# Block-diagonal gate products of a recurrent mixer: two products a tile instead of three, and an earlier place in TensorE's queue

## What is computed

```python
def rglru_mixer(x, w_in, conv_w, conv_b, w_a, b_a, w_x, b_x, a_param, w_out):
    z = x @ w_in
    gate_branch, xb = z[..., :D_RNN], z[..., D_RNN:]
    xp = jnp.pad(xb, ((0, 0), (CONV_WIDTH - 1, 0), (0, 0)))
    xc = conv_b + conv_w[0] * xp[:, 0:S]
    for k in range(1, CONV_WIDTH):
        xc = xc + conv_w[k] * xp[:, k:k + S]
    xh = xc.reshape(B, S, LRU_HEADS, LRU_HEAD_DIM)
    r = jax.nn.sigmoid(jnp.einsum('bshi,hij->bshj', xh, w_a).reshape(B, S, D_RNN) + b_a)
    ig = jax.nn.sigmoid(jnp.einsum('bshi,hij->bshj', xh, w_x).reshape(B, S, D_RNN) + b_x)
    log_a = -LRU_C * r * jax.nn.softplus(-a_param)
    a = jnp.exp(log_a)
    mult = jnp.sqrt(-jnp.expm1(2.0 * log_a))
    bterm = mult * (ig * xc)
    _, h = lax.associative_scan(_lin_combine, (a, bterm), axis=1)
    y = h * jax.nn.gelu(gate_branch)
    return y @ w_out
```

## Time and profile before

| | |
|---|---|
| median of three executions | 1741.39 us |
| the profiled execution, its own time | 1741.45 us |
| its span, first to last instruction | 1739.6 us |
| mean granted TensorE clock | 0.999 |
| PE busy | 1728.8 us (99%), 9535 matmul instructions |
| PE weight load busy | 1500.2 us (86%) |
| DVE busy | 1262.9 us (73%) |
| ACT busy | 1003.7 us (58%) |
| POOL busy | 58.9 us (3%) |
| moved by DMA | 311.65 MB, mean 179 GB/s |

### The profile page before, as it was taken

One profiled execution on the slowest core, in us unless ns is written; L12 is line 12 of the kernel. 1 busy time (PEld: TensorE's weight loads), 2 busy tenths in 40 slices (PEclk: granted clock), 3 DMA queues, 4 the chain that ended last, 5 costly groups with the idle time before them and its releaser, 6 DMA issues.

```text
span 1739.6 us, 24239 instructions
## 1 busy us (share of the span) xinstructions
PE 1728.8 (99%) x9535; PEld 1500.2 (86%) x9535; DVE 1262.9 (73%) x1602; ACT 1003.7 (58%) x1247; POOL 58.9 (3%) x95
## 2 busy tenths in 40 slices
PE   9999999999999999999999999999999999999998
PEld 8888998888888888888889888888888988888887
DVE  6766777766677666876667898867666898876665
ACT  7544566654467444754457866464446966565444
POOL 7200000000000000000001000000000000000000
PEclk9999999999999999999999999999999999999999
DMA  7755435665545655465545544356555554446552
GB/s 244 255 189 188 162 122 170 217 222 189 191 169 181 212 187 176 144 208 185 189 145 194 184 165 145 122 186 220 190 192 170 163 176 134 138 165 215 188 186 88
DMA packets 211564, 311.65 MB, mean 179 GB/s; under 512 B 6434, under 2 KB 166112, under 8 KB 211360
## 3 DMA queue, kind: packets, MB, share of 16 engines
q1 hardware_dynamic: 207472, 303.84, 53.4%
q0 software_dynamic: 3712, 6.44, 1.2%
q10 hardware_dynamic: 304, 0.33, 0.1%
HBM read 309.54 MB, written 1.05 MB: 179 GB/s over the span
## 4 chain that ended last, share of the span: by engine, by line
PE 91%; ACT 4%; DVE 3%; issue 1%; DMA 0%; SPq 0%; DVEq 0%; ACTq 0%
PE psD L1945 28%; PE psA L1834 27%; PE psA L1839 14%; PE psA L1912 3%; PE psA L1927 3%; PE psA L1778 3%; PE psA L1945 2%; PE psD L2231 2%; PE psA L1931 1%; PE psA L1916 1%; PE psA L1783 1%; PE psA L2015 1%; ACT hi L455 1%; PE psD L2168 1%; PE psD L2015 1%
## 5 line engine op out<-in xcount | busy, mean ns | idle before, releaser
L927 DVE TENSOR_TENSOR lo<-raw,hi 128x2048 fp32r<-128x2048 f32 x285 | 650.5, 2290 | 171.9 <-ACT hi L455 171.2
L455 ACT ACTIVATE hi<-raw 128x2048 fp32r<-128x2048 f32 x285 | 542.4, 1909 | 77.2 <-PE psD L1945 33.5
L1834 PE MATMUL psA<-xT,hi 128*128 128x512 f32 x2094 | 501.1, 390 | 0.1
L1834 PEld LDWEIGHTS psA<-xT,hi 128*128 128x128 f32 x2094 | 387.2, 188 | 77.0 <-DVE xT L960 0.3
L1839 PEld LDWEIGHTS psA<-xT,lo 128*128 128x128 f32 x2112 | 271.9, 191 | 11.8 <-issue 0.5
L1839 PE MATMUL psA<-xT,lo 128*128 128x256 f32 x2112 | 276.8, 283 | 0.1
L1945 PE MATMUL psD<-hi,prod_hi 128*128 128x512 f32 x544 | 213.4, 392 | 0.0
L1945 PE MATMUL psD<-hi,prod_lo 128*128 128x512 f32 x544 | 212.6, 391 | 0.0
L1945 PE MATMUL psD<-lo,prod_hi 128*128 128x512 f32 x544 | 143.6, 389 | 0.0
L593 ACT ACTIVATE scr<-psA 128x512 f32<-128x512 f32 x66 | 39.3, 595 | 163.3 <-PE psA L1839 163.3
L608 ACT ACTIVATE prod_hi<-scr 128x512 fp32r<-128x512 f32 x66 | 41.7, 632 | 157.8 <-DVE scr L1309 157.8
(11 more groups left out here) (308 smaller groups left out, 1926.2 us busy)
## 6 DMA issues: line engine op xcount, KB each, us to landing
raw<-in_w_in SPq DMA_DIRECT2D x48, 1024.0 KB, 5.2
raw<-in_ffn_w_up SPq DMA_DIRECT2D x43, 1024.0 KB, 5.4
raw<-in_ffn_w_gate SPq DMA_DIRECT2D x43, 1024.0 KB, 5.4
raw<-in_ffn_w_down SPq DMA_DIRECT2D x43, 1024.0 KB, 5.0
raw<-in_w_gate SPq DMA_DIRECT2D x22, 1024.0 KB, 5.3
raw<-in_w_up SPq DMA_DIRECT2D x22, 1024.0 KB, 5.3
raw<-in_w_down SPq DMA_DIRECT2D x22, 1024.0 KB, 4.9
raw<-in_lru_w_in SPq DMA_DIRECT2D x10, 1024.0 KB, 5.3
```

The source lines that it names most:

```text
L455: act.activation(hi[:, n % RING, :], raw_of(n), ACT.Copy).then_inc(hi_ready, 1)
L927: dve.tensor_tensor(lo[:, n % RING, :], raw_of(n), hi[:, n % RING, :].bitcast(F32), ALU.subtract).then_inc(lo_ready, 1)
L1834: pe.matmul(psA[:, bank + f, :], w_hi[:, k, f * P:(f + 1) * P], xT[:, k].rearrange("p e s -> p (e s)"), start=(k == 0), stop=False)
```

## The change

The band now holds, for each output tile, two sets of rows instead of three. The product of the tile with itself stands in one set (parity m % 2), and in the other set lie the blocks of both neighbours, in one 128-row weight: a head's block keeps the rows at which its input features lie, and these are the lower partitions for the tile above and the upper partitions for the tile below. The moving operand for it is `cross`, a copy of `xc` whose partitions 64 to 127 come from the tile before and 0 to 63 from the tile behind. It is made by ACT's DMA queue, from on-chip memory to on-chip memory, in two parts for each group (`cross_rows(g, part)`: two copies of 64 partitions; part 0 for output tiles 1 and 2, part 1 for tile 3), and each waits for the tiles of the convolution that it reads. The end tiles of a group have one neighbour only: their second product reads `xc` itself, 64 rows of it (0 to 63 of the tile behind, or 64 to 127 of the tile before). So each tile takes two products for each gate, 20 a group.

PE runs group 0 behind feature block 4 (the fifth) and group 1 behind block 5 (the sixth), each tile with its own wait for `xc_ready` in place of one for the group. ACT's and DVE's programs are put into another order with it, and the GELU of the first four tiles now stands behind the decay of group 1. On DVE the scan is separate from `recur`. POOL zeroes 5120 columns instead of 7680.

```diff
@@ pool
-            band = view(BAND, 2, 2, GT, 384)
-            pool.memset(scr[:, BAND:BAND + 2 * 2 * GT * 384], 0.0).then_inc(band_zeroed, 1)
+            band = view(BAND, 2, 2, 2, GT * P)
+            pool.memset(scr[:, BAND:CROSS], 0.0).then_inc(band_zeroed, 1)
...
-                        pool.dma_start(band[part:part + cnt, m, g, tile, col:col + HD],
+                        pool.dma_start(band[part:part + cnt, m, g, tile % 2, head * HD:(head + 1) * HD],
@@ scalar
+                    xc, cross = view(L_XC, RT, S), view(CROSS, 2, 3, S)
+
+                    def cross_rows(g, part):
+
+                        k0, k1 = ((0, 2), (2, 3))[part]
+                        act.wait_ge(xc_ready, GT * g + k1 + 2)
+                        act.dma_start(cross[P // 2:P, g, k0:k1, :], xc[P // 2:P, g * GT + k0:g * GT + k1, :]).then_inc(cross_landed[g][part], 16)
+                        act.dma_start(cross[0:P // 2, g, k0:k1, :], xc[0:P // 2, g * GT + k0 + 2:g * GT + k1 + 2, :]).then_inc(cross_landed[g][part], 16)
...
-                        if i == half + 2:
+                        n += 1
+                        if i == half - 1:
+                            cross_rows(0, 0)
+                            cross_rows(0, 1)
+                            recurrent_gates(0)
+                            cross_rows(1, 0)
+                            half_tanh(0)
+                        if i == half:
+                            cross_rows(1, 1)
+                            recurrent_decay(0)
+                            recurrent_gates(1)
                             half_tanh(1)
-                        if i == half + 3:
+                        if i == half + 1:
                             recurrent_decay(1)
-                        n += 1
-                        if i == half:
-                            recurrent_gates(0)
-                            half_tanh(0)
-                        if i == half + 1:
-                            recurrent_decay(0)
                             gelus(0, 4)
-                            recurrent_gates(1)
@@ vector
                     def recur(g):
 
                         gs = slice(g * GT, (g + 1) * GT)
+                        settle()
                         dve.wait_ge(gates_ready, 2 * GT * (g + 1))
...
-                        if g == 1:
-                            split_to(n + 1)
-                            dve.wait_ge(block_used, n + 2)
-                            rows_in(2 * half - 1)
+
+                    def scan(g):
+
                         settle()
...
                     for i in range(2 * half):
+                        if i >= half + 3:
+                            evacuate(i)
                         split_to(n)
...
-                        if 1 <= i < 2 * half - 1:
+                        if i == half + 2:
+                            for c in range(2):
+                                piece(xc[:, 2 * c:2 * c + 2, :], c)
+                        if 1 <= i < half + 3:
                             evacuate(i)
                         if 1 <= i < half:
                             convolve(i)
+                        if i == half:
+                            recur(0)
+                            scan(0)
                         if i == half + 1:
-                            recur(0)
+                            recur(1)
                             dve.wait_ge(gelu_ready, 1)
                             outputs(0, 2)
                         if i == half + 2:
-                            for c in range(2):
-                                piece(xc[:, 2 * c:2 * c + 2, :], c)
-                        if i == half + 3:
-                            recur(1)
+                            scan(1)
@@ tensor
                     def recurrent_gates(g):
 
-                        pe.wait_ge(xc_ready, GT * (g + 1))
                         for m in range(GT):
                             ft = g * GT + m
+                            pe.wait_ge(xc_ready, GT * g + min(m + 2, GT))
                             if ft >= 4:
                                 pe.wait_ge(gates_ready, 2 * (ft - 3))
+                            if 0 < m < GT - 1:
+                                pe.wait_ge(cross_landed[g][m // 3], 32)
+                                beside = cross[:, g, m - 1, :]
+                            else:
+                                beside = xc[:, g * GT + (1 if m == 0 else m - 1), :]
+                            ms = slice(m * P, (m + 1) * P)
+                            rows_ = slice(0, P // 2 if m == 0 else P) if m < GT - 1 else slice(P // 2, P)
                             for e in range(2):
-                                ks = [k for k in (m - 1, m, m + 1) if 0 <= k < GT]
-                                for k in ks:
-                                    last = pe.matmul(psD[:, ft % 4, e * S:(e + 1) * S], band[:, e, g, k, (m - k + 1) * P:(m - k + 2) * P],
-                                                     xc[:, g * GT + k, :], start=(k == ks[0]), stop=(k == ks[-1]))
+                                bank = psD[:, ft % 4, e * S:(e + 1) * S]
+                                pe.matmul(bank, band[:, e, g, m % 2, ms], xc[:, ft, :], start=True, stop=False)
+                                last = pe.matmul(bank, band[rows_, e, g, (m + 1) % 2, ms], beside[rows_, :], start=False, stop=True)
                             last.then_inc(gates_done, 1)
...
-                        if i == half:
+                        if i == half - 1:
                             pe.wait_ge(band_loaded, 16 * 2 * 2 * len(head_pieces()))
                             recurrent_gates(0)
-                        if i == half + 1:
+                        if i == half:
                             recurrent_gates(1)
```

More of the change, by code:

```diff
@@ L65 @@
 BAND = L_IG + RT * S
+CROSS = BAND + 2 * 2 * 2 * R // 2
 POOL_M, POOL_B, POOL_S = 4096, 6144, 7168
@@ L75 @@
 SCRATCH = 22784
-assert BAND + 2 * 2 * GT * 384 <= SCRATCH
+assert CROSS + 2 * 3 * S <= SCRATCH
 def head_pieces():
@@ L151, in build @@
         band_zeroed, band_loaded = sem("band_zeroed"), sem("band_loaded")
+        cross_landed = [[sem(f"cross_landed{g}{part}") for part in range(2)] for g in range(2)]
         p_loaded, pool_loaded, mix_loaded = sem("p_loaded"), sem("pool_loaded"), sem("mix_loaded")
@@ L353, in _ @@
                 for head, row, tile, part, cnt in head_pieces():
-                    col = head * HD - (tile - 1) * P
                     for g in range(2):
-                        pool.dma_start(band[part:part + cnt, m, g, tile, col:col + HD],
+                        pool.dma_start(band[part:part + cnt, m, g, tile % 2, head * HD:(head + 1) * HD],
                                        w[8 * g + head, row:row + cnt, :]).then_inc(band_loaded, 16)
@@ L2155, in _ @@
                     half = R // FC
-                    band, xc = view(BAND, 2, 2, GT, 384), view(L_XC, RT, S)
+                    band, xc, cross = view(BAND, 2, 2, 2, GT * P), view(L_XC, RT, S), view(CROSS, 2, 3, S)
                     def recurrent_gates(g):
-                        pe.wait_ge(xc_ready, GT * (g + 1))
                         for m in range(GT):
                             ft = g * GT + m
+                            pe.wait_ge(xc_ready, GT * g + min(m + 2, GT))
                             if ft >= 4:
                                 pe.wait_ge(gates_ready, 2 * (ft - 3))
+                            if 0 < m < GT - 1:
[5 more added lines that the diff above has]
+                            rows_ = slice(0, P // 2 if m == 0 else P) if m < GT - 1 else slice(P // 2, P)
                             for e in range(2):
-                                ks = [k for k in (m - 1, m, m + 1) if 0 <= k < GT]
-                                for k in ks:
-                                    last = pe.matmul(psD[:, ft % 4, e * S:(e + 1) * S], band[:, e, g, k, (m - k + 1) * P:(m - k + 2) * P],
-                                                     xc[:, g * GT + k, :], start=(k == ks[0]), stop=(k == ks[-1]))
+                                bank = psD[:, ft % 4, e * S:(e + 1) * S]
+                                pe.matmul(bank, band[:, e, g, m % 2, ms], xc[:, ft, :], start=True, stop=False)
+                                last = pe.matmul(bank, band[rows_, e, g, (m + 1) % 2, ms], beside[rows_, :], start=False, stop=True)
                             last.then_inc(gates_done, 1)
```

## The result

The change made the kernel slower: 1743.93 us median of 20 executions (1740.74 to 1745.23) against 1741.07 before in the same series (1740.54 to 1741.88), ratio 1.0014 with a 95% interval of 1.0008 to 1.002. That lies inside the range of the forecast (1738.6 to 1744.4) and within the 0.2% that it called no change, but the step is beyond the measurement's interval and goes the other way than 1740.8. It is the rival in which the clock falls, 1743.7. The profiled execution took 1744.29 us, span 1742.5.

A forecast was written before the change was run, and what follows sets the result against it. PE, holding 91% of the span, was taken as the bound, with ACT meeting it at tile 9. Gains of 5.18 - 0.7 us, mostly spent waiting there, left 0.65: 1741.45 - 0.65 = 1740.8 us, range 1738.6 to 1744.4.

The forecast's parts named there:

- the rival in which the clock falls: PE's gap at tile 9 brings back half pace, losing 2.9 us: 1743.7 us; chance 22%.
- What bounds the kernel, and ACT at tile 9: PE holds 91% of the span; PE and ACT reach tile 9 together, so moving PE forward alone meets ACT.
- Part 1: Gate products on PE: 80 instructions instead of 104, at 0.216 us each, 5.18 us less.
- Part 2: Eight 64-row products in the end tiles: each 0.08 us over a 128-row one, 0.7 us in all.
- Part 3: Gate groups moved forward: PE waits about 4 us at tile 9, and the first output product starts 0.65 us earlier.
- the release: At tile 9, ACT's sigmoids of tile 5 free the bank for PE at 251.0 us.
- the sum: Profiled execution of 1741.45 us less 0.65 gives 1740.8 us, with bounds of 1739.2 to 1742.3.
- Parts 4 and 5: Copies on ACT's queue land in time, and loads, splits and POOL's zeroing change nothing: no time for either.
- The other two rivals: No wait at tile 9: 1736.6 us, chance 12%; first copies landing late for tile 1: 1746.3 us, chance 8%.

The follow-up runs named there:

- e3: The changed kernel with ACT's tanh of group 0 ahead of the copies that wait for DVE's last convolution; 1739.77 us.
- e1: The changed kernel with the end tiles' second products reading all 128 rows, the other 64 weight rows being zeros; 1743.02 us.
- e11: The changed kernel with unread 64-row test products ahead of the wait; eight instructions took 1.99 us on one half of the rows, 1.14 on two halves.
- e2: The changed kernel with nine products that nothing reads ahead of PE's wait at tile 9; 1741.28 us.
- e8: e5 with ACT's sigmoids of tile 5 ahead of the decay of group 0; 1738.27 us.
- e6: e3 with each tile's two products with itself first, then its two with its neighbours; 1739.42 us in one execution.
- e7: The changed kernel with four products that nothing reads ahead of PE's wait at tile 9; 1741.25 us.
- e10: The changed kernel with 128 rows in the neighbour products of tile 9 alone; 1741.76 us.
- e5: The changed kernel with the edits of e3 and e1 together; 1738.98 us.
- e4: The kernel before with the new products and copies, both groups at their old places, ACT and DVE in their old order; 1746.76 us.

## Why the prediction was wrong

**What bounds the kernel, and ACT at tile 9: right.** PE's one wait stands where it was forecast, for the instruction that was forecast, released at 250.88 where I had 251.0. e3 shows that ACT's order is its cause.

**Part 1, 80 instructions at 0.216: right** by the trace of e1, where 128-row products start 0.43 us apart (two instructions each) and a group of 20 takes 8.6 us.

**Part 2, the 64-row products: the term was mis-sized.** I had +0.08 us for each over one of 128 rows, 0.7 for eight, since I read the scores' rows as one product's two instructions side by side. The pairs that start together are two products on different halves (e11). Measured, an end tile takes 2.40 against 1.73, so +0.34 each; with the delay that it leaves to the next tile (0.54 from 227.52 to 228.06, for 0.43) it is +0.39, which is also e1's 2.36 us for six, and 3.1 for eight. My upper end was +0.29. The two rules of the Trainium skill that I had weighed against the rows, "TensorE: Matmul & The Clock Gate", on why this matters (small K alone gains nothing, only different tiles at once do), and "TensorEngine Tiling (Array Packing)", Key Properties (a change of mode drains), were both right here: together they gave a product at the 128-row price plus the switches, for which I had 0.29 and 0.39 is measured, and I set the first one aside for a row that did not show what I took it to show. For the time at the full clock this step was nearly harmless, since PE came to tile 9 at 248.75 instead of 247.05 and merely waited less, 2 us instead of 4. Only tile 9's own share reached the end: 2.51 us in e2 (250.04 to 252.55) where I had 2.0.

**Part 3, the release and the sum: right but for the clock.** With the clock held up by filling work, e2 took 1741.28, against the 1740.8 of the sum, and three runs of the changed kernel at 0.999 took 1740.74, 1740.82 and 1741.11. That the release was met within 0.1 us is partly luck: of the four issues the second pair ran beside the tanh and cost ACT nothing, and the first pair took 0.47 and 0.61 us instead of 0.35 each; the two errors nearly cancel.

**Parts 4 and 5: right.** The copies landed in time, 2.3 and 2.0 us behind their issue. Groups of the changed kernel's DMA issues:

```profile
scr<-scr ACTq DMA_DIRECT2D x4, 128.0 KB, 2.3
...
scr<-scr ACTq DMA_DIRECT2D x4, 64.0 KB, 2.0
```

No block waited for a split. In e8, where PE is further ahead, it waits 1.37 us for one.

**The rivals: this is the step that failed.** The sum put the clock at nothing behind the new wait and left its fall to a rival with a chance of 22%; it comes in 16 of 20 runs. The rival had the right place and price (1743.7 for 1743.93), so the change of direction, slower instead of 0.6 us faster, is this one term. I held the gap of 4 us that I forecast to be short beside 80 us of unbroken work. Even one of 2 us was not, and the work ahead of it did not protect. The low stretch of 6.8 us is a little longer than the 5.9 of the program's start that I had priced; it cost 3.0 us where I had 2.9. The other two rivals did not come.

How often and how long it falls, over all kernels with a wait at tile 9:

| kernel | wait, us | products behind it | runs with a fall | low in the profiled run, us |
|---|---|---|---|---|
| e6 | 0.95 | 64-row | 0 of 1 | none |
| e7 | 0.97 | 64-row | 1 of 10 | none |
| changed | 1.96 | 64-row | 16 of 20 | 6.8 |
| e10 | 1.96 | 128-row | 6 of 11 | 3.4 |
| e5 | 2.31 | 128-row | 3 of 11 | 3.4 |
| e4 | 3.50 | 64-row | 7 of 7 | 10 |
| e1 | 4.32 | 128-row | 10 of 11 | 3.4 |

So after waits of 2 us the fall is a matter of chance, and after those over 3 us it came in 17 of 18 runs. e8's wait of 1.37 us ahead of a feature block brought none in 10. 64-row products behind the wait make the low stretch longer: e10 shows it for one exchange of products at the same wait. Whether they also make the fall likelier is not shown. Neither is why they lengthen it, and they are not the only thing that does, since e1 has 128-row products and a mean clock of 0.997 in 5 of 11 runs.

## What to carry to other kernels

Where one engine works without a break, taking work from it is worth something only if the engine that it meets next is early enough: follow that one first. Count every new wait of TensorE of 2 us or more with the clock's fall behind it, before calling a gain spent or kept. Here it cost 1.4 us (e5) to 3.2 us (the changed kernel), the medians of runs with a fall less those without. Then look for the one line in the other engine's order that stands behind a wait it doesn't need. A product of 64 rows was no saving here; it was one only where its neighbour in the queue worked on the other 64 (and, in these runs, into another bank).

## What the runs showed of the hardware that I had not expected

An idle time of 2 us in a stage that is otherwise unbroken brought TensorE to 1.2 GHz in 16 of 20 executions. In the profiled runs of the changed kernel, e1, e5 and e10 it fell 0.5 to 1.1 us after work had resumed; in e4, behind 3.5 us of idleness, 0.6 us before. The same kernel therefore scatters over 4.5 us (1740.74 to 1745.23) where the one before scatters over 1.3. Filling the wait with products that nothing reads is worth 2.65 us (e2), and with less than half of the filling the same (e7).
